# First block of a group reads the moved low part in place, and the first down group takes its columns in the order 3, 2, 0, 1

## The reference

```python
def swiglu(x, w_gate, w_up, w_down):          # x: rows x 1024, hidden width 2816
    g = jnp.einsum("btd,df->btf", x, w_gate)
    up = jnp.einsum("btd,df->btf", x, w_up)
    return jnp.einsum("btf,fd->btd", jax.nn.silu(g) * up, w_down)
```

## Time and profile before

| | us |
|---|---|
| median of 3 runs | 1606.38 (1604.79 to 1607.85) |
| profiled execution, its own time | 1607.32 |
| its span, from first to last instruction | 1605.60 |
| PE busy / POOL busy / DVE busy / ACT busy | 1587.2 / 706.6 / 992.1 / 562.4 |
| PE in the chain that ended last | 93% |
| mean granted clock of TensorE | 0.996 |

### The profile page before, as it was taken

How to read it: one execution, slowest core, us unless ns; L and a number is a source line. 1 busy time by engine, 2 the same in 40 slices (tenths; PEclk the granted TensorE clock), 3 DMA queues, 4 the chain that set the end, 5 groups by cost and what they waited for, 6 DMA issues and landing times.

```text
span 1605.6 us, 30062 instructions
## 1 busy us (share of the span) xinstructions
PE 1587.2 (99%) x12361; PEld 1537.8 (96%) x12361; DVE 992.1 (62%) x1371; ACT 562.4 (35%) x868; POOL 706.6 (44%) x521
## 2 busy tenths in 40 slices
PE   9999999999999999999999999999999999999998
PEld 6889999999999999999978999999999999999998
DVE  7757856586683337768865664544444456575755
ACT  4222332222223335334435432222222234353544
POOL 1011534554544444545730334444444444464675
PEclk9999999999999999999999999999999999999999
DMA  6202011431423333574423313533333347473723
GB/s 224 71 1 80 27 53 34 126 100 40 126 86 108 107 106 119 162 226 141 149 84 131 118 53 93 153 120 94 100 113 101 101 143 210 145 238 106 238 106 133
DMA packets 155843, 187.27 MB, mean 117 GB/s; under 512 B 7404, under 2 KB 138084, under 8 KB 155452
## 3 DMA queue, kind: packets, MB, share of 16 engines
q1 hardware_dynamic: 152635, 182.41, 35.9%
q10 hardware_dynamic: 3072, 2.95, 0.6%
HBM read 133.74 MB, written 48.72 MB: 114 GB/s over the span
## 4 chain that ended last, share of the span: by engine, by line
PE 93%; DVE 2%; issue 2%; DMA 1%; POOL 1%; SPq 0%; ACT 0%; POOLq 0%; DVEq 0%; ACTq 0%
PE ps L438 89%; PE ps L473 1%; PE ps L550 1%; DMA pre_gain<-in_mix_pre_g 1%; DMA tp_f<-hid_dram 1%; PE ps L726 0%; PE ps L710 0%; PE ps L448 0%; DVE tp L2325 0%; POOL ring_lo L1157 0%; SPq L832 0%; POOL ring_lo L1170 0%; DVE tp L2495 0%; DVE s_bc L2344 0%; POOL x_late L1229 0%
## 5 line engine op out<-in xcount | busy, mean ns | idle before, releaser
L438 PE MATMUL ps<-tp,ring_hi 128*128 128x258 f32 x7248 | 1179.2, 284 | 9.2 <-POOL ring_lo L1157 5.2
L438 PEld LDWEIGHTS ps<-tp,ring_hi 128*128 128x128 f32 x7248 | 1007.5, 190 | 10.4 <-POOL ring_lo L1157 5.6
L438 PE MATMUL ps<-tp,ring_lo 128*128 128x258 f32 x3624 | 741.8, 283 | 0.0
L438 PEld LDWEIGHTS ps<-tp,ring_lo 128*128 128x128 f32 x3624 | 569.3, 191 | 0.0
L1157 POOL TENSOR_TENSOR ring_lo<-ring_f,ring_hi 128x512 fp32r<-128x512 f32 (+1 forms) x240 | 343.7, 1452 | 348.0 <-DVE ring_f L1973 212.6
L1157 POOL TENSOR_TENSOR ring_lo<-stage,ring_hi 128x512 fp32r<-128x512 f32 (+1 forms) x196 | 288.6, 1480 | 418.9 <-ACT ring_hi L1302 418.5
L1302 ACT ACTIVATE ring_hi<-ring_f 128x512 fp32r<-128x512 f32 (+1 forms) x240 | 150.0, 625 | 508.1 <-DVE ring_f L1968 169.9
L1302 ACT ACTIVATE ring_hi<-stage 128x512 fp32r<-128x512 f32 (+1 forms) x196 | 120.5, 618 | 234.9 <-PE ps L438 161.4
L1965 DVE TENSOR_TENSOR ring_f<-stage 128x512 f32<-128x512 f32 (+1 forms) x60 | 56.7, 944 | 108.3 <-DMA stage<-in_w_in 52.4
L438 PE MATMUL ps<-tp 128*128 128x512 f32 (+1 forms) x384 | 72.0, 340 | 0.0
L438 PEld LDWEIGHTS ps<-tp 128*128 128x128 f32 x384 | 59.0, 189 | 8.2
(11 more groups left out here) (269 smaller groups left out, 1423.7 us busy)
## 6 DMA issues: line engine op xcount, KB each, us to landing
stage<-in_w_in SPq DMA_DIRECT2D x24, 1024.0 KB, 6.0
ht_dram<-ht SPq DMA_DIRECT2D x44, 258.0 KB, 4.7
hid_dram<-hq SPq DMA_DIRECT2D x40, 258.0 KB, 3.1
stage<-in_w_gate SPq DMA_DIRECT2D x10, 1024.0 KB, 7.3
stage<-in_w_up SPq DMA_DIRECT2D x10, 1024.0 KB, 5.4
tp_f<-ht_dram SPq DMA_DIRECT2D x16, 516.0 KB, 6.8
stage<-in_w_down SPq DMA_DIRECT2D x8, 1024.0 KB, 5.3
tp_f<-hid_dram SPq DMA_DIRECT2D x12, 516.0 KB, 8.8
```

The costliest lines, as they stand in the source:

```text
L438: ins = pe.matmul(o, w, xc, start=first and n == 0, stop=last and n == 2, skip_group_check=onto)
```

## The change

PE's product 1 of a group's first block reads the low part where it was made (`early_lo`) and waits for the high part of its slot and for `early_done`. The wait for the move goes to product 1 of the group's second block. `early_move` goes behind the split of product 4's operand. A table `D_COLUMNS = [3, 2, 0, 1]` gives the columns of a group's four blocks, for all three groups (weight loads, `c11_down`, `down_rest`, the squares at the end follow it). The waits for the places in `g` go to the blocks that now write them, three of the four hidden totals and their waits go behind c22 of block B_D, and the store of the last totals goes behind the load of block B_D + 2's weights. The load of `early2` waits also for product 1 of block B_D + 4, which reads that place now.

```diff
+D_COLUMNS = [3, 2, 0, 1]
...
                     if p == 1:
-                        pe.wait_ge(early_moved, 32 * (n + 1))
+                        pe.wait_ge(early_done, n + 1)
+                        pe.wait_ge(t_hi, 7 * n + 2)
                     else:
                         pe.wait_ge(t_lo, t_lo_at(n, p))
+                elif b in (B_D + 1, B_D + MP + 1, B_D + 2 * MP + 1) and p == 1:
+                    pe.wait_ge(early_moved, 32 * ((b - B_D) // MP + 1))
...
+                x_hi, x_lo = tp[:, s, 0], tp[:, s, 1]
+                if p == 1 and b in (B_D, B_D + MP, B_D + 2 * MP):
+                    x_lo = early_lo[(b - B_D) // MP]
...
                 if b + 2 < B_END and not last:
                     load(b + 2)
+                if b == B_D:
+                    spill_totals(J - 1)
...
                     spill_hidden(j, 3)
-                    spill_totals(j)
+                    if j < J - 1:
+                        spill_totals(j)
...
                         sp.wait_ge(early_moved, 64)
+                        sp.wait_ge(prod_done, done(FIRST_RUN[B_D + MP], 1))
...
                 if n == 1:
+                    for t in range(4):
+                        act.wait_ge(ht_saved[t], 16 * (MP + J))
                     c11_down(r)
                 t_split(n, 1)
                 prepare(nb, 2, 3)
                 t_split(n, 2)
-                early_move(n)
                 prepare(nb, 3, 5)
                 t_split(n, 3)
                 s1(r + 1)
                 prepare(nb, 5, 6)
                 t_split(n, 4)
+                early_move(n)
                 prepare(nb, 6)
...
                         if mp:
                             prepare(b + 1, 0, 3)
-                            for n in range(4):
-                                act.wait_ge(ht_saved[n], 16 * (MP + J))
-                        else:
+                        if mp == 1:
+                            act.wait_ge(early_moved, 32)
+                        elif mp == 2:
                             act.wait_ge(hid_saved[0], 16 * J)
-                            act.wait_ge(ht_ready, 4 * MP + 4 * (J - 1) + 1)
+                            act.wait_ge(ht_ready, 4 * MP + 4 * J)
                         c11_down(r)
```

More of the change, by code:

```diff
@@ L366, in y_event @@
             if e < 12:
-                return 2 * (e // 4) + a, b, both
-            return 2 * (MP - 1) + a, b, only[(e - 12) // 4]
+                return 2 * D_COLUMNS[e // 4] + a, b, both
+            return 2 * D_COLUMNS[MP - 1] + a, b, only[(e - 12) // 4]
         consts = sem("consts")
@@ L627, in issue @@
                 w_h, w_l = w_ring(b, p)
+                x_hi, x_lo = tp[:, s, 0], tp[:, s, 1]
+                if p == 1 and b in (B_D, B_D + MP, B_D + 2 * MP):
+                    x_lo = early_lo[(b - B_D) // MP]
                 for kp in range(kps(b)):
                     ins = three(outs, w_h[:, kp], w_l[:, kp],
-                                *([tp[:, s, part, n, kp, 0:CS] for n in range(gs.start, gs.stop)] for part in range(2)),
+                                *([x[:, n, kp, 0:CS] for n in range(gs.start, gs.stop)] for x in (x_hi, x_lo)),
                                 kp == 0 and p not in (2, 6), kp == kps(b) - 1, p in (2, 6))
@@ L848, in load @@
                 else:
-                    src = columns(w_down[0], 256 * ((b - B_D) % MP), 2 * K_FIRST[(b - B_D) // MP], 2 * kps(b))
+                    src = columns(w_down[0], 256 * D_COLUMNS[(b - B_D) % MP], 2 * K_FIRST[(b - B_D) // MP], 2 * kps(b))
                 if b in RAW_SLOT:
@@ L1700, in c11_down @@
             def c11_down(r):
-                c11_act(r, g[:, 2 * (RUNS[r][0] - B_D), 0], ACT.Copy).then_inc(c11_copied, 1)
+                c11_act(r, g[:, 2 * D_COLUMNS[RUNS[r][0] - B_D], 0], ACT.Copy).then_inc(c11_copied, 1)
             def t_begin(n, r, nb):
@@ L2578, in down_rest @@
                 run = r - FIRST_RUN[B_D + MP]
-                m, parts = 2 * ((b - B_D) % MP), 3 * run
+                m, parts = 2 * D_COLUMNS[(b - B_D) % MP], 3 * run
                 nb = b + 1 if r < R_LAST else None
@@ L2640, in _ @@
             for b in range(B_D, B_D + MP):
-                r, m, mp = FIRST_RUN[b], 2 * (b - B_D), b - B_D
-                if mp:
-                    sums(b + 1, 0)
-                if mp == MP - 1:
-                    t_rest(1, 0)
+                r, m, mp = FIRST_RUN[b], 2 * D_COLUMNS[b - B_D], b - B_D
                 if mp == 0:
                     t_rest(0, 5)
-                    u2(r)
+                sums(b + 1, 0)
+                if mp == 1:
+                    dve.wait_ge(early_moved, 32)
+                elif mp == 2:
+                    for n in (1, 2, 3):
+                        dve.wait_ge(hid_saved[n], 16 * J)
+                    dve.wait_ge(ht_ready, 4 * MP + 4 * J)
+                elif mp == 3:
+                    for n in range(4):
+                        dve.wait_ge(ht_saved[n], 16 * (MP + J))
+                    t_rest(1, 0)
+                u2(r)
+                u4(r, g[:, m, 1])
+                sums(b + 1, 1)
+                if mp == 0:
+                    t_rest(0, 6)
+                c22(r, g[:, m + 1, 1], g[:, m, 1])
+                if mp == 0:
                     hidden_total(J - 1, 0, hq)
-                    sums(b + 1, 0)
                     hidden_total(J - 1, 2, hq)
-                    dve.wait_ge(ht_ready, 4 * MP + 4 * (J - 1) + 2)
-                    dve.wait_ge(hid_saved[1], 16 * J)
-                    u4(r, g[:, m, 1])
-                    sums(b + 1, 1)
-                    hidden_total(J - 1, 1, hq)
-                    t_rest(0, 6)
-                    dve.wait_ge(ht_ready, 4 * MP + 4 * (J - 1) + 3)
-                else:
-                    if mp == 1:
-                        for n in range(4):
-                            dve.wait_ge(ht_saved[n], 16 * (MP + J))
-                    u2(r)
-                    u4(r, g[:, m, 1])
-                    sums(b + 1, 1)
-                if mp == 0:
-                    dve.wait_ge(hid_saved[3], 16 * J)
-                c22(r, g[:, m + 1, 1], g[:, m, 1])
                 sums(b + 1, 2)
@@ L2675, in _ @@
                 sums(b + 1, 3)
-                if mp == MP - 1:
-                    t_rest(1, 3)
                 if mp == 0:
+                    hidden_total(J - 1, 1, hq)
                     dve.wait_ge(hid_ready, 4 * (J - 1))
                     hidden_total(J - 1, 3, hq)
-                    dve.wait_ge(ht_ready, 4 * MP + 4 * J)
-                    dve.wait_ge(hid_saved[2], 16 * J)
+                elif mp == 3:
+                    t_rest(1, 3)
                 c21(r, g[:, m + 1, 0])
```

## The result

| | before | change |
|---|---|---|
| median of the runs compared | 1606.3 (1604.79 to 1607.85, 4 runs) | 1594.86 (1594.62 to 1595.33, 4 runs) |
| profiled execution, its own time | 1607.32 | 1594.81 |
| its span | 1605.60 | 1593.1 |
| PE busy | 1587.2 | 1583.8 |
| PE in the chain that ended last | 93% | 97% |

The change is faster: the ratio of its time to that before is 0.9929, with a 95% interval of 0.9914 to 0.9944. The medians stand 11.4 us apart, the profiled executions 12.5. The forecast was 1595.4 with a range of 1592.5 to 1599.5. The kernel before spreads widely, from 1603.2 us at a mean granted clock of 0.999 to 1610.0 at 0.995 over the executions of all jobs; the change stays between 1594.5 and 1595.3 at 0.999 to 1.0.

A forecast was written before the change was run, and what follows sets the result against it. PE bounds the kernel, busy 1587.2 of 1605.60 us. Losses of 12.7 us less new waits of 0.7, 1.0 and 0 give 11.0 us less: 1606.38 - 11.0 = 1595.4 us, range 1592.5 to 1599.5.

The forecast's parts named there:

- the change misses the wait: Rival, chance 0.03: POOL is the releaser, 7.9 us of losses at blocks B_D + 4 and B_D + 8 stay; 1602.3 us.
- The sum of the losses, 12.7 us: PE's waits and lower-clock matmuls around blocks B_D, B_D + 4 and B_D + 8 lose 12.7 us, all targeted.
- New waits, 1.7 us in all: Waits the change would bring: 0.7 us in block B_D, 1.0 before product 5 of B_D + 4, 0 at B_D + 8.
- Place 1: Block B_D: waits of 0.36 us for u2 and 2.96 for c22, plus 1.5 by the lower clock; loses 4.8 us.
- I take half, 1.1 us: Block B_D: product 5's data land 1.1 us earlier, half of the move's 2.3 us, as the move goes behind the split.
- Place 2: Product 1 of block B_D + 4: a wait of 3.61 us for the move, plus 2.7 by the lower clock; loses 6.3 us.
- I take 0.7 us of the 3.0, which leaves a wait of 1.0 us: Block B_D + 4: product 5's data land 0.7 us earlier, cutting its wait for u2 from 1.7 to 1.0 us.
- Product 6's data, landed at 1433.09, are due only near 1439 and fit.: Block B_D + 4: product 6's data, landed at 1433.09, are in time for its need near 1439.
- Place 3: Product 1 of block B_D + 8: a 1.62 us wait for the move, no slow matmuls; loses 1.6 us, no new wait.
- Equal turns: Rival, chance 0.20: the move shares DMA rate evenly from its issue; new waits cost 3.4 us, 9.3 less, 1597.1 us.
- DVE is late: Rival, chance 0.10: hidden totals behind c22 make block B_D + 1 wait 3 us, lowering the clock; 7.2 less, 1599.2 us.
- The data of product 5 come last: Rival, chance 0.06: the move on ACT's queue delays SP's loads; landings 4 us later give 4.2 more, 1610.6 us.

The follow-up runs named there:

- columns and order only: The change with product 1 of a group's first block again reading the moved low part and waiting for the move, issued at its old place: 1603.85 us.
- the kernel with both edits: The change with the move issued behind product 6's split and DVE's c22 add put ahead of product 6's operand rest: 1594.89 us.
- the one with the add ahead alone: The change with DVE's c22 add put ahead of product 6's operand rest in down groups 1 and 2: 1593.85 us.

## Why the prediction was right, and where it was not

The time came out 0.5 us below the forecast, and each of the three places lost roughly what the prediction said it would. That the two times are so near is in part luck: for the profiled execution the prediction had 1607.32 - 11.0 = 1596.3, and it took 1594.8. The forecast carried the losses of one execution of the kernel before over to its median, although they vary with the clock. Step by step:

- *PE waits for the move, not for POOL* ("So PE waits for the move"). Right. The wait is gone with the read in place alone, and it comes back with the move's own name when it is asked for. The rival "the change misses the wait" falls.
- *The sum of the losses, 12.7 us.* The three waits are gone and so is the lower clock at places 1 and 2. PE's busy time fell by 3.4 us, where the prediction's two clock terms give 1.5 + 2.7 = 4.2 and its last part said "some 4 us". By the same matmul in both traces the places give 5.4, 6.4 and 1.9 us (4.8, 6.3 and 1.6 in the prediction), 0.9 more than its sum. Part of this is how a wait is listed: PE loses 0.2 to 0.5 us more by a wait than the profile's figure for it, in the change 1.0 for 0.71 and in the read in place alone 2.2 for 1.74.
- *New waits, 1.7 us in all.* Too much: 0.7 were found, 1.0 by the same matmul. With the item above, the change won 12.6 us in this stretch where the prediction has 11.0.
- *Place 1, "I take half, 1.1 us" for the landing of product 5's data.* This step failed in size: they landed 3.0 us earlier. That u2 was still ready at 1363.7, where the estimate has 1363.9, is two errors that cancel. The rest began at 1360.07 and not at 1360.9, held by product 4's rest on DVE and no longer by the data, and it took 2.59 us and not the 1.77 that the prediction costed. The weight sum took 0.55, c22 came at 1366.53 (estimated end 1367.8 to 1369.2, measured 1367.2), and PE had no wait. The 0.7 us taken for place 1 was 0.
- *Place 2, "I take 0.7 us of the 3.0, which leaves a wait of 1.0 us" before product 5.* Failed as well. In the change's rows the data are at 1423.09; before they were at 1430.18, which is 1424.9 with the 5.3 us by which all is earlier there: 1.8 earlier, and no wait for u2. With the move at its old place the wait of 1.55 us is there, so the term was the right one and only its size was wrong. The prediction had the move share the rate from its issue on. It sent its first packet only 4.0 us later, and 0.50 of its 1.06 MB ahead of those data: the other 0.56 MB are 1.6 us at 351 GB/s, near the 1.8 measured.
- *"Product 6's data, landed at 1433.09, are due only near 1439 and fit."* This is where the wait really was. The data did fit. The prediction costed DVE's work behind product 5's data with durations of rows that had nothing beside them, and did not list DVE's work behind product 6's data, the add of line 2610 above all. It took 1.80 us and not 0.69, and 0.7 of the 1.1 reached PE. The trace of before had this already, at the same step, where PE did not have to wait for it (L2597 there is line 2610 now):

```profile
1441.32 1.79 DVE L2597 TENSOR_TENSOR g<-g,s_bc 128x516 f32<-128x516 f32 x1
```

  That the total at place 2 (1.0 taken, 0.7 found) nearly agrees is luck.
- *Place 3, no wait.* Right.
- *Equal turns.* The equal share was right from the move's first packet on, and wrong for the 4.0 us before it. So the case is not what the change does: it has neither of its waits. The kernel with the move at its old place has two of like size (1.59 and 1.55 us, where the case has 0.9 and 1.9 for u2), by another mechanism: the whole move ahead of the data, and at place 1 a slow weight sum. *DVE is late* did not come: the totals behind c22 ended in time for block B_D + 1. *The data of product 5 come last* did not either; they came earlier.
- *The chances.* "Faster by over 0.2% is all but the last two rivals" miscounts: the rival that misses the wait has 4.1 us less, which is over 3.2, and half of the last one is within it. The result falls under "faster" either way.

The expectations of the first runs erred on the same two points: the one for columns and order only left out that without the later move product 5 waits again (1.46 us), and that a wait a quarter of a microsecond longer than the old 1.62 could bring the clock down.

What stays open: at place 1 the move's traffic does not explain the whole landing. 0.31 MB of its 0.79 went between 1352.5 and 1357.4, and the other 0.48 are 1.4 us, where the data landed 3.0 earlier. SP's own issue moved as well: it issued the second of these loads at 1350.8 us in the change and at 1351.9 with the move at its old place. That is 1.1 us more; whether the two add up, no run tests. Why the kernel with both edits, its add ahead of the rest, still ends 1.0 us behind the one with the add ahead alone is read from DVE and POOL's rows only; no run with POOL's order changed was made.

## What to carry to other kernels

When a consumer waits for a copy of something that already lies in the memory it can read, let it read the original and put the copy behind the loads that are needed sooner; here the read was worth 4.8 us alone, and the place of the copy about 3 us of what the whole change won. On the engine that feeds the critical one, list every instruction between the last input and the value waited for, and put what needs no late input ahead of what does. And look at what the neighbour engine does at that time before costing it: bringing data forward by 3 us won nothing where it only moved DVE's work beside POOL's.

## What the runs showed of the hardware that was not expected

**DVE and POOL in each other's way.** A DVE add of 128x516 values with both inputs in SBUF took 1.80 us beside a POOL instruction and 0.69 with POOL idle, and a rest of 128x2064 values 3.41 and 2.30. DVE instructions of the same shape that read PSUM stayed at 0.68 to 0.70 beside POOL (1434.03 in the change, with POOL busy from 1433.33). POOL's instructions grow too: 2.39 us at 1430.98, against 1.29 at 1423.96. The long add began at 1432.12 and ended at 1433.92, 0.55 us behind the POOL instruction that ended at 1433.37; it looks as if it stood still until then. The reverse stands in the kernel with the add ahead: the rest began at 1429.95, before POOL's instruction at 1430.84, and took its 2.30 us, and POOL's took 2.57. The Trainium skill ("SBUF — State Buffer", section "SBUF: two separate sides") says that a DVE instruction with two SBUF inputs and a GpSimd one that reads SBUF lock a shared port pair for their whole length, and whichever comes second is blocked. These rows agree with that.

**A DMA that starts late beside another queue's work.** The move's first packet came 4.0 us after its issue at place 2, while SP's queue had all of the rate, and from then on the two queues sent alike (0.52 and 0.50 MB in 2.9 us). The same delay was 3.1 us at place 1, and 3.6 and 3.9 in the kernel before. With the move behind product 6's split SP's queue sent nothing when it was issued: the first packet came after 1.2 us, and the two transfers landed 3.3 and 4.6 us after their issue. In the kernel with both edits SP issued weights at the same moment as the move, 1425.6 us. There the first packet came after 3.5 us and the landings took 7.4 and 8.2, although SP's queue moved only 148 GB/s in that time and the engines were not full. So it is not the rate alone that held the packets back; what did, these runs don't show.

**The clock behind short waits.** In the down part of all these traces the granted clock stayed up behind PE waits of 0.7 to 1.74 us (ten of them) and fell behind those of 1.86, 2.19, 2.96, 3.61, 4.28 us and longer. The lower clock lasted 3.4 us behind the waits of 1.86, 2.19, 2.96, 2.97 and 4.28 us, of which half is lost, 6.8 us at the wait of 3.61, and 10.2 us at each of the three waits of 6.5 to 10.3 us. At the long waits it fell before the wait had ended (at 1357.65 us in a wait until 1361.80, at 1429.33 in one until 1436.33), so only what is left of it behind the wait slows matmuls: 6.1, 3.2 and 5.1 us, of which half is lost. So the wait of 1.86 us cost about twice its length here (3.6 us by the same matmul), and the one of 1.74 cost 2.2. What the clock goes by beyond this, these runs don't show.
